# Hybrid decoder block on one core: the order of state output, query rotation and z products, and 64-row matmuls of two group halves taken in turn

## The chip, the cores and the metric

One core of a Trainium2 chip runs the whole program. The metric is the device time of one execution in microseconds; the kernel before was executed three times. Engines are named as in the profile: PE is TensorE (PEld its weight loads), DVE is VectorE, ACT is ScalarE, POOL is GpSimd, SP is SyncE, which here only issues DMA.

## What is computed

One layer over 1024 tokens of width 1024, with two parallel token mixers, in float32:

```
h = rms_norm(x) * (1 + scale) + shift
q | kv(cmp, slc, win) | nsa gates | z_attn | u | z_ssm | merge gates = h @ w_in
A = NSA(rope(q), kv) * silu(z_attn)      # compressed + selected + window attention, 8 heads, 2 KV groups
S = GLU(gelu(S5(u))) * silu(z_ssm)       # 16 SSM groups of 16 channels, 64 complex states each
m = sigmoid(m_a) * (A @ w_proj_attn) + sigmoid(m_s) * (S @ w_proj_ssm)
out = rms_norm(x + gate * (m @ w_out))
```

S5 is a diagonal complex recurrence. The kernel computes it in chunks of 8 tokens: lag kernels (`klag`) give what a token takes from its own chunk, and a scan over 128 chunks gives the state that a chunk starts from. The output y of a group is the state part (real and imaginary) plus the part from within the chunk (a Toeplitz matrix `toep` built from the lags).

## The kernel before, in words

Every engine has its own instruction list, and semaphores tie them together. An engine works its list strictly in order, so the place of a step in the list decides what it can delay. The projections `h @ w_in` are cut into nine weight chunks (U_, ZS_, Q0_, Q1_, KC_, Z0_, KS_, KW_, Z1_, line 56) and eight token tiles of 128 rows. One such unit is 24 matmuls (three products of a high/low split over 8 slices of the width) into one of the banks 4 to 7, and a unit waits until the unit four places before it has been read.

The middle of the program runs in this order on PE: `ZS_`, six tiles of `Q0_`, the lag kernels (lines 1714 to 1724), transposes of the input matrices into `gt` (1726), the last two tiles of `Q0_`, the chunk inputs `bu` (1736), `Q1_`, and then the list `KC_ORDER` (466): units of KC_ and Z0_, mixed with `y` (`lag_outputs`, 1748), its transposes `yt`, key transposes `kc` and the GLU. Fills of banks 0 and 1 are counted: fill n waits (`fill_free`) until the one two places before it has been evicted, which ACT reports on `s_trf`.

In the lag kernels and in y a group pair lies on the partitions: half `gp` = 0 on rows 0 to 63, half 1 on rows 64 to 127. The fp32 matmuls of a fill all use one half, and the profile shows two records for each matmul.

- ACT evicts klag (904), gt, then `b_r` and `b_i` (919 to 926). `b_i` shares its memory with klag, so it waits for the `toep` transfers that SP issues once POOL has added the skip term (`lags`, 716 to 721). Later ACT evicts y to `ytok` (932) and works `KC_READS` (983): values of the KC_ tiles, Gelus of the transposed y, and so on.
- DVE rotates the queries (`rotate_queries`, two heads and half of the tiles a call) for b = 0 and 1 ahead of the state chain (`states`, 1237) and for b = 2 and 3 behind it. `states` is a chain of products of 128x1024 and sixteen scans; with its sixth step lies the low part of the KC_ weights. Its last instruction signals `rot`, on which PE waits for y. `kc_keys` comes behind the last rotation and behind y.
- POOL splits the Z0_ weights (`split_w(5)`, 731) as soon as ACT has their high part.

The attention stage is a written list of steps (`opening_plan`, 135, and `attention_plan`, 149) which every engine works through, each doing its own part of a step. In the opening, `GS` is ACT's sigmoid of the gates, `Z i` the unit i of Z1_ with ACT's silu into `zs`, `KT` key transposes with ACT's and DVE's evictions, `MQ 0` the query transposes of head 0 and ACT's copies into `q1`, `PQ` ACT's scaled copy of a head's queries and POOL's duplicate, `PL` their low part on DVE, `MX` and `MW` the row maxima. `MX` needs `q1` and z unit 1. Per head there are six results (branch br, half cc, r = 2 br + cc). DVE forms each (`ND`); for r of 2 and more POOL adds it into `qa` (783). After every eight of these sums, that is after heads 1, 3 and 5, POOL multiplies a pair of heads with silu(z), 128x1024 (784 to 788). Its queue also holds the low part of the weights of the compressed branch (770).

```
KC_ORDER = [("P", KC_, 0), ("P", KC_, 1), ("y",), ("P", KC_, 2), ("yt", 0), ("yt", 1), ("P", KC_, 3),
...
KC_READS = [step for step in KC_ORDER if step != ("P", KC_, 4)]
KC_READS.insert(KC_READS.index(("kc", 3)) + 1, ("P", KC_, 4))
```

Of the kernel before, what the change touches and what calls it, by code (L numbers as in the profile page):

```python
# [22 lines left out]
P = 128  # L23
SEQ = 1024
D_MODEL = 1024
KT = D_MODEL // P
# [17 lines left out]
CH = 8  # L44
# [90 lines left out]
def opening_plan():  # L135


    def pair(i):
        return [("MX", 0, i), ("MW", 0, i)]
    plan = [("GS",), ("Z", 0, 0, KT), ("KT", 2 * ST - 2), ("KT", 2 * ST - 1), ("PL", 0), ("MQ", 0, 0), ("MQ", 0, 1),  # L140
            ("PQ", 1), ("Z", 1, 0, KT)]
    for i in range(ST):
        plan += pair(i) + [("Z", 2 + i // 2, 4 * (i % 2), 4 * (i % 2) + 4)]
    plan += [("MC", 0, p) for p in range(4)]
    plan += [("Z", 6, 0, KT), ("MM", 0, 0), ("Z", 7, 0, KT), ("MM", 0, 1), ("PL", 1)]
    return plan
# [57 lines left out]
def build(nc, x, c, w_ada, b_ada, norm_gain, w_in, pe_cmp_k, w_cmp_k1, b_cmp_k1, w_cmp_k2,  # L204
# [258 lines left out]
    for n, name in enumerate(FILLS):  # L463
        first.setdefault(name, n)

    KC_ORDER = [("P", KC_, 0), ("P", KC_, 1), ("y",), ("P", KC_, 2), ("yt", 0), ("yt", 1), ("P", KC_, 3),
                ("yt", 2), ("yt", 3), ("P", KC_, 4), ("kc", 0), ("kc", 1), ("glu", 0), ("kc", 2), ("kc", 3),
# [14 lines left out]
    with nc.Block() as block:  # L482
# [114 lines left out]
        def _(pool):  # L597
# [128 lines left out]
            def split_w(w):  # L726

                n = CHUNKS[w][1]
                pool.wait_ge(s_whi, w + 1)
                tt(wlo[w % 2][:, :, 0:n], wraw[:, :, 0:n], f(whi[w % 2][:, :, 0:n]), ALU.subtract).then_inc(s_wlo, 1)  # L730
            split_w(5)
# [19 lines left out]
            for step in [("PQ", 0)] + plan:  # L751
# [20 lines left out]
                elif step[0] == "ND" and step[2] == 3 and step[1] % 6 >= 2:  # L772
# [11 lines left out]
                    if n_sum % 8 == 0 and n_sum < 4 * HEADS:  # L784
                        pool.wait_ge(once("norm"), n_sum)
                        b = n_sum // 8 - 1
                        tt(qa[:, b, :, :], qa[:, b, :, :], zs[:, :, P * b:P * b + P], ALU.mult).then_inc(once("az"), 1)
                        pool.wait_ge(once("az"), b + 1)
# [22 lines left out]
        def _(act):  # L811
# [92 lines left out]
            for q in range(4):  # L904
                gp, th = divmod(q, 2)
                bk = fill(first["klag"] + q)
                a(kl[:, gp, 4 * th:4 * th + 4, :], bk[0:SC, :].rearrange("p (t s) -> p t s", t=4)).then_inc(s_trf, 1)
# [24 lines left out]
            for q in range(4):  # L932
                bk = fill(first["y"] + q)
                if q == 0:
                    act.wait_ge(once("rot"), 1)
                gp, th = divmod(q, 2)
# [199 lines left out]
        def _(dve):  # L1136
# [123 lines left out]
            for b in range(2):  # L1260
                for hf in range(2):
                    rotate_queries(b, slice(4 * hf, 4 * hf + 4))
# [5 lines left out]
            for b in range(2, 4):  # L1268
# [315 lines left out]
        def _(pe):  # L1584
# [129 lines left out]
            for q in range(4):  # L1714
                gp, th = divmod(q, 2)
                n = first["klag"] + q
                fill_free(n)
                s = slice(SS * gp, SS * gp + SS)
                for m in range(4):
                    t = 4 * th + m  # L1720
                    for r in range(2):
                        ins = mm(bank[n % 2][0:SC, P * m:P * m + P], bbar[r][s, t, :],
                                 cp[r][s, t, 0:CH, :].rearrange("p j c -> p (j c)"), r == 0, r == 1)
                ins.then_inc(s_tr, 1)
# [23 lines left out]
            def lag_outputs():  # L1748
# [3 lines left out]
                for q in range(4):  # L1752
                    n = first["y"] + q
                    fill_free(n)
                    gp, th = divmod(q, 2)
                    s = slice(SS * gp, SS * gp + SS)
                    for m in range(4):
                        t = 4 * th + m
                        g = 2 * t + gp
                        o = bank[n % 2][:, P * m:P * m + P]  # L1760
                        for r, st in enumerate((zr, zi)):
                            mm(o, st[s, t, :], cp[r][s, t, 1:9, :].rearrange("p j c -> p (j c)"), r == 0, False)
                        ins = mm(o, ut[:, g, :], toep[:, g, :], False, True)
                    ins.then_inc(s_tr, 1)
# [238 lines left out]
            for step in plan:  # L2003
                if step == ("N", 6 * HEADS - 1):
# [3 lines left out]
                    for n in range(6):  # L2008
                        b, hf = divmod(n, 2)
                        pe.wait_ge(once("az"), b + 1)  # L2010
# [95 lines left out]
```

## Time and profile before

| what | value |
|---|---|
| median of 3 runs | 1028.67 us (1028.46 to 1030.15) |
| the profiled execution | 1029.62 us, its span 1027.7 us |
| PE busy | 943.4 us, 92% of the span |
| DVE, ACT, POOL busy | 529.9, 395.5, 213.3 us |
| mean granted TensorE clock | 0.963 |
| chain that ended last, by engine | PE 74%, DVE 14%, ACT 8%, issue 3% |

The span runs from the first to the last instruction. The chain of the last row follows the program back from its end: at each step to what released the instruction, or to the one before it on its engine. A granted clock of 1.00 is 2.4 GHz, 0.50 is 1.2 GHz. Times in the rows are microseconds from the start of the span.

### The profile page before, as it was taken

Reading aid. Unit: us, or ns where it says so; the run is one execution under the profiler, and the core shown is the slowest. Engines: PE = TensorE matmul, PEld = TensorE weight load, DVE = VectorE, ACT = ScalarE, POOL = GpSimd, SP = SyncE. Lnnn points to the kernel's source line nnn. Section 1 sums busy time; section 2 is a strip of 40 time slices with the busy share of each in tenths; the row PEclk is TensorE's granted clock in tenths of the full one; section 3 lists DMA queues with packets and bytes.
Section 4 is the critical chain, followed back from the end, with each engine's and each line's share of the span. In section 5 each row is a group of like instructions: output and inputs, shape, how many; then the busy total and the mean of one; then the engine's idle time right before and its main releaser. Section 6 shows DMA issues by size and latency. Waiting matters only on the chain.

```text
span 1027.7 us, 14338 instructions
## 1 busy us (share of the span) xinstructions
PE 943.4 (92%) x5581; PEld 770.2 (75%) x5581; DVE 529.9 (52%) x1075; ACT 395.5 (38%) x786; POOL 213.3 (21%) x204
## 2 busy tenths in 40 slices
PE   0799998999998989989989989879999999998996
PEld 0488997879998966666767666568888888886885
DVE  1652198134685466877867868562123122217453
ACT  5542231233114167667666675751111111105121
POOL 6259411012010012122021131135553000000000
PEclk9899997599999999999999999989999999999999
DMA  9916041004110000000000000032332222042322
GB/s 319 327 59 106 7 104 62 1 1 86 41 43 1 1 1 2 1 1 1 2 1 1 1 1 5 27 105 72 96 84 60 57 57 57 1 163 87 119 82 82
DMA packets 53714, 59.66 MB, mean 58 GB/s; under 512 B 10096, under 2 KB 45488, under 8 KB 52608
## 3 DMA queue, kind: packets, MB, share of 16 engines
q1 hardware_dynamic: 51392, 54.13, 17.7%
q0 software_dynamic: 2000, 4.54, 1.6%
q8 instruction: 44, 0.72, 0.3%
q14 instruction: 22, 0.18, 0.1%
q10 hardware_dynamic: 256, 0.09, 0.0%
HBM read 52.92 MB, written 5.24 MB: 57 GB/s over the span
## 4 chain that ended last, share of the span: by engine, by line
PE 74%; DVE 14%; ACT 8%; issue 3%; DMA 1%; POOL 0%; ACTq 0%; DVEq 0%
PE bank L1588 42%; PE slc_max L1588 15%; PE win_max L1588 13%; PE bank L1591 3%; DVE plo L1141 3%; DVE mx L1410 2%; ACT pt L815 1%; DVE mx L1417 1%; ACT phi L815 1%; ACT osb L815 1%; DVE zi L1141 1%; DVE rt L1141 1%; ACT L815 1%; ACT junk L815 1%; DMA prow<-in_lam_im 1%
## 5 line engine op out<-in xcount | busy, mean ns | idle before, releaser
L1141 DVE TENSOR_TENSOR plo<-pt,phi 128x512 fp32r<-128x512 f32 x192 | 117.1, 626 | 40.1 <-ACT phi L815 39.7
L815 ACT ACTIVATE pt<-bank 128x512 f32<-128x512 f32 (+1 forms) x208 | 98.7, 475 | 92.1 <-PE bank L1588 91.0
L1588 PE MATMUL bank<-q,k 128*128 128x512 f32 (+7 forms) x384 | 104.0, 353 | 0.9
L815 ACT ACTIVATE phi<-bank 128x512 fp32r<-128x512 f32 (+1 forms) x208 | 98.4, 473 | 0.0
L601 POOL TENSOR_TENSOR qa<-qa,otmp 128x256 f32<-128x256 f32 x32 | 27.7, 865 | 221.4 <-DVE otmp L1141 221.4
L1588 PEld LDWEIGHTS bank<-q,k 128*128 128x128 f32 (+1 forms) x384 | 64.3, 192 | 12.3 <-ACT phi L815 3.3
L1588 PE MATMUL bank<-phi,vhi 128*65 128x512 f32 x192 | 71.0, 370 | 2.3 <-ACT osb L815 1.9
L1588 PE MATMUL bank<-phi,vlo 128*64 128x512 f32 x192 | 62.9, 328 | 0.0
L1588 PE MATMUL bank<-plo,vhi 128*65 128x512 f32 x192 | 62.9, 328 | 0.0
L1410 DVE TENSOR_REDUCE mx<-slc_max 128x1 f32<-128x128 f32 (+3 forms) x64 | 48.1, 752 | 13.1 <-PE slc_max L1588 13.1
L1588 PE MATMUL bank<-ht_hi,dhi 128*128 128x512 f32 x128 | 51.0, 398 | 2.4 <-DVE at_lo L1141 2.4
L1588 PE MATMUL bank<-ht_hi,dlo 128*128 128x512 f32 x128 | 50.8, 397 | 0.0
L1588 PE MATMUL bank<-ht_lo,dhi 128*128 128x512 f32 x128 | 50.8, 397 | 0.0
L815 ACT ACTIVATE dsig<-bank 128x512 f32<-128x512 f32 x16 | 9.6, 599 | 106.3 <-PE bank L1588 106.3
L1588 PE MATMUL bank<-whi,ht_hi 128*128 128x256 f32 (+1 forms) x160 | 47.9, 299 | 0.0
L1588 PE MATMUL bank<-wlo,ht_hi 128*128 128x256 f32 (+1 forms) x160 | 46.4, 290 | 0.0
L1588 PE MATMUL win_max<-whi,ht_hi 128*128 128x256 f32 (+1 forms) x160 | 46.3, 290 | 0.0
L1588 PE MATMUL bank<-whi,ht_lo 128*128 128x256 f32 (+1 forms) x160 | 46.3, 289 | 0.0
L1588 PE MATMUL win_max<-wlo,ht_hi 128*128 128x256 f32 (+1 forms) x160 | 45.4, 284 | 0.0
L1588 PE MATMUL win_max<-whi,ht_lo 128*128 128x256 f32 (+1 forms) x160 | 45.2, 283 | 0.0
L1417 DVE TENSOR_REDUCE mx<-win_max 128x1 f32<-128x640 f32 (+2 forms) x64 | 41.5, 648 | 0.0
L1141 DVE TENSOR_TENSOR mt<-bank,dsig 128x512 f32<-128x512 f32 x8 | 5.5, 692 | 64.4 <-ACT dsig L815 54.4
(385 smaller groups left out, 2595.8 us busy)
## 6 DMA issues: line engine op xcount, KB each, us to landing
ada<-in_w_ada SPq DMA_DIRECT2D x8, 1024.0 KB, 17.3
draw<-in_w_in SPq DMA_DIRECT2D x16, 512.0 KB, 3.9
wraw<-in_w_in SPq DMA_DIRECT2D x7, 1024.0 KB, 6.0
xs<-in_x SPq DMA_DIRECT2D x8, 512.0 KB, 11.1
gstage<-in_w_ada POOLq DMA_DIRECT2D x16, 256.0 KB, 3.1
oraw<-in_w_out SPq DMA_DIRECT2D x8, 512.0 KB, 6.6
xr<-in_x SPq DMA_DIRECT2D x8, 512.0 KB, 4.3
out<-yr SPq DMA_DIRECT2D x8, 512.0 KB, 2.9
```

Of the source, the lines that this page charges most:

```text
L601: return nc.gpsimd.tensor_tensor(o, a, b, op)
L815: return nc.scalar.activation(o, i, fn, **kw)
L1141: return V.tensor_tensor(o, a, b, op)
L1410: V.tensor_reduce(m[:, i, 1:2], slc_max[:, 0:P * (i + 1)], AX.X, ALU.max).then_inc(once("msr"), 1)
L1417: V.tensor_reduce(m[:, i, 2:3], win_max[:, 0:P * min(i + 1, WIN_TILES + 1)], AX.X, ALU.max)\
L1588: return T.matmul(o, l, r, start=start, stop=stop, **kw)
L1591: return T.transpose(o, i, ident[0:rows, 0:rows])
```

## The change

- `KC_ORDER`: y comes after three KC_ tiles instead of two, and its transposes one tile later too.
- POOL waits for `rot` before it splits the Z0_ weights.
- DVE rotates only b = 0 ahead of the states, and b = 1 to 3 behind them.
- Lag kernels and y: the two halves gp take turns, instruction by instruction, and each half and th has a bank of its own (0 to 3). ACT evicts in the new order. In y the eight 128-row matmuls with `toep` follow the sixteen 64-row ones of their th.
- POOL's z product is done in pieces of 128x256, each right behind a window sum (r of 4 and 5) of heads 0 to 5.
- Opening: z unit 1 comes before the query steps of head 0.

```diff
--- before.py
+++ after.py
@@ -137,8 +137,8 @@
 
     def pair(i):
         return [("MX", 0, i), ("MW", 0, i)]
-    plan = [("GS",), ("Z", 0, 0, KT), ("KT", 2 * ST - 2), ("KT", 2 * ST - 1), ("PL", 0), ("MQ", 0, 0), ("MQ", 0, 1),
-            ("PQ", 1), ("Z", 1, 0, KT)]
+    plan = [("GS",), ("Z", 0, 0, KT), ("KT", 2 * ST - 2), ("KT", 2 * ST - 1), ("PL", 0), ("Z", 1, 0, KT), ("MQ", 0, 0),
+            ("MQ", 0, 1), ("PQ", 1)]
     for i in range(ST):
         plan += pair(i) + [("Z", 2 + i // 2, 4 * (i % 2), 4 * (i % 2) + 4)]
     plan += [("MC", 0, p) for p in range(4)]
@@ -463,8 +463,8 @@
     for n, name in enumerate(FILLS):
         first.setdefault(name, n)
 
-    KC_ORDER = [("P", KC_, 0), ("P", KC_, 1), ("y",), ("P", KC_, 2), ("yt", 0), ("yt", 1), ("P", KC_, 3),
-                ("yt", 2), ("yt", 3), ("P", KC_, 4), ("kc", 0), ("kc", 1), ("glu", 0), ("kc", 2), ("kc", 3),
+    KC_ORDER = [("P", KC_, 0), ("P", KC_, 1), ("P", KC_, 2), ("y",), ("P", KC_, 3), ("yt", 0), ("yt", 1), ("P", KC_, 4),
+                ("yt", 2), ("yt", 3), ("kc", 0), ("kc", 1), ("glu", 0), ("kc", 2), ("kc", 3),
                 ("P", KC_, 5), ("glu", 1), ("P", KC_, 6), ("glu", 2), ("P", KC_, 7), ("glu", 3),
                 ("P", Z0_, 0), ("kc", 4), ("kc", 5), ("P", Z0_, 1), ("kc", 6), ("kc", 7)]
     KC_ORDER += [("P", Z0_, i) for i in range(2, ST)]
@@ -728,6 +728,7 @@
                 n = CHUNKS[w][1]
                 pool.wait_ge(s_whi, w + 1)
                 tt(wlo[w % 2][:, :, 0:n], wraw[:, :, 0:n], f(whi[w % 2][:, :, 0:n]), ALU.subtract).then_inc(s_wlo, 1)
+            pool.wait_ge(once("rot"), 1)
             split_w(5)
 
             for n in range(4):
@@ -781,11 +782,10 @@
                     n_sum += 1
                     dst = qa[:, h // 2, 4 * cc:4 * cc + 4, HD * (h % 2):HD * (h % 2) + HD]
                     tt(dst, dst, otmp[:, :, :], ALU.add).then_inc(once("norm"), 1)
-                    if n_sum % 8 == 0 and n_sum < 4 * HEADS:
+                    if r >= 4 and h < HEADS - 2:
                         pool.wait_ge(once("norm"), n_sum)
-                        b = n_sum // 8 - 1
-                        tt(qa[:, b, :, :], qa[:, b, :, :], zs[:, :, P * b:P * b + P], ALU.mult).then_inc(once("az"), 1)
-                        pool.wait_ge(once("az"), b + 1)
+                        tt(dst, dst, zs[:, 4 * cc:4 * cc + 4, HD * h:HD * h + HD], ALU.mult).then_inc(once("az"), 1)
+                        pool.wait_ge(once("az"), 2 * h + cc + 1)
 
             pool.wait_ge(once("norm"), 4 * HEADS)
             for n in range(2 * KT):
@@ -902,9 +902,9 @@
                 query_tile(Q0_, i)
             kl = klag[:, :, :].rearrange("p (t g) s -> p g t s", g=2)
             for q in range(4):
-                gp, th = divmod(q, 2)
-                bk = fill(first["klag"] + q)
-                a(kl[:, gp, 4 * th:4 * th + 4, :], bk[0:SC, :].rearrange("p (t s) -> p t s", t=4)).then_inc(s_trf, 1)
+                th, gp = divmod(q, 2)
+                fill(first["klag"] + q)
+                a(kl[:, gp, 4 * th:4 * th + 4, :], bank[q][0:SC, :].rearrange("p (t s) -> p t s", t=4)).then_inc(s_trf, 1)
             for q in range(4):
                 r, th = divmod(q, 2)
                 bk = fill(first["gt"] + q)
@@ -930,10 +930,11 @@
                 query_tile(Q1_, i)
             split_w(Z0_)
             for q in range(4):
-                bk = fill(first["y"] + q)
+                fill(first["y"] + q)
+                bk = bank[q]
                 if q == 0:
                     act.wait_ge(once("rot"), 1)
-                gp, th = divmod(q, 2)
+                th, gp = divmod(q, 2)
                 yv = ytok[:, :, :].rearrange("p j (t g c) -> p g t j c", g=2, c=SC)
                 a(yv[:, gp, 4 * th:4 * th + 4, :, :], bk.rearrange("p (t j c) -> p t j c", t=4, c=SC)).then_inc(s_trf, 1)
 
@@ -1257,15 +1258,14 @@
                 yield ch.link(tt(zI, zI, eC, ALU.mult))
                 yield tt(zI, zI, bI, ALU.add).then_inc(once("rot"), 1)
 
-            for b in range(2):
-                for hf in range(2):
-                    rotate_queries(b, slice(4 * hf, 4 * hf + 4))
+            for hf in range(2):
+                rotate_queries(0, slice(4 * hf, 4 * hf + 4))
             dve.wait_ge(s_trf, first["bu"] + 4)
             dve.wait_ge(once("ecos"), 1)
             for n, _ in enumerate(states()):
                 if n == 6:
                     split_w(KC_)
-            for b in range(2, 4):
+            for b in range(1, 4):
                 for hf in range(2):
                     rotate_queries(b, slice(4 * hf, 4 * hf + 4))
 
@@ -1711,17 +1711,15 @@
             project(Q0_, range(6))
             pe.wait_ge(once("cp"), 1)
             pe.wait_ge(s_eva, UU)
-            for q in range(4):
-                gp, th = divmod(q, 2)
-                n = first["klag"] + q
-                fill_free(n)
-                s = slice(SS * gp, SS * gp + SS)
+            for th in range(2):
                 for m in range(4):
                     t = 4 * th + m
                     for r in range(2):
-                        ins = mm(bank[n % 2][0:SC, P * m:P * m + P], bbar[r][s, t, :],
-                                 cp[r][s, t, 0:CH, :].rearrange("p j c -> p (j c)"), r == 0, r == 1)
-                ins.then_inc(s_tr, 1)
+                        for gp in range(2):
+                            s = slice(SS * gp, SS * gp + SS)
+                            ins = mm(bank[2 * th + gp][0:SC, P * m:P * m + P], bbar[r][s, t, :],
+                                     cp[r][s, t, 0:CH, :].rearrange("p j c -> p (j c)"), r == 0, r == 1)
+                ins.then_inc(s_tr, 2)
             pe.wait_ge(once("gs"), 2)
             for q in range(4):
                 r, th = divmod(q, 2)
@@ -1749,19 +1747,20 @@
 
                 pe.wait_ge(once("rot"), 1)
                 pe.wait_ge(once("toep"), 16 * CH)
-                for q in range(4):
-                    n = first["y"] + q
-                    fill_free(n)
-                    gp, th = divmod(q, 2)
-                    s = slice(SS * gp, SS * gp + SS)
+                pe.wait_ge(s_trf, first["y"])
+                for th in range(2):
                     for m in range(4):
                         t = 4 * th + m
-                        g = 2 * t + gp
-                        o = bank[n % 2][:, P * m:P * m + P]
                         for r, st in enumerate((zr, zi)):
-                            mm(o, st[s, t, :], cp[r][s, t, 1:9, :].rearrange("p j c -> p (j c)"), r == 0, False)
-                        ins = mm(o, ut[:, g, :], toep[:, g, :], False, True)
-                    ins.then_inc(s_tr, 1)
+                            for gp in range(2):
+                                s = slice(SS * gp, SS * gp + SS)
+                                mm(bank[2 * th + gp][:, P * m:P * m + P], st[s, t, :],
+                                   cp[r][s, t, 1:9, :].rearrange("p j c -> p (j c)"), m == 0 and r == 0, False)
+                    for gp in range(2):
+                        for m in range(4):
+                            g = 2 * (4 * th + m) + gp
+                            ins = mm(bank[2 * th + gp][:, P * m:P * m + P], ut[:, g, :], toep[:, g, :], False, m == 3)
+                        ins.then_inc(s_tr, 1)
 
             def lag_transposes(q):
 
@@ -2007,7 +2006,7 @@
                     pe.wait_ge(once("exp"), 2 * HEADS * NU)
                     for n in range(6):
                         b, hf = divmod(n, 2)
-                        pe.wait_ge(once("az"), b + 1)
+                        pe.wait_ge(once("az"), 4 * (b + 1))
                         for q in range(4):
                             ins = tr(bank[n][:, P * q:P * q + P], qa[:, b, 4 * hf + q, :])
                         ins.then_inc(once("att"), 1)
```

## Rows read from the trace of the kernel before

**Rows 1.** PE in order of time, the state outputs y (start, us, engine, line, operation).

```profile
166.13 0.48 PE L1588 MATMUL bank<-cp,zr 64*128 64x128 f32 x2 [4.29 <-DVE zi L1141]
...
171.36 0.79 PE L1588 MATMUL bank<-cp,zr 64*128 64x128 f32 x2
...
173.23 0.79 PE L1588 MATMUL bank<-cp,zr 64*128 64x128 f32 x2
```

**Rows 2.** DVE in order of time, state chain, rotations, first two KC_ tiles.

```profile
138.95 1.23 DVE L1141 TENSOR_TENSOR zr<-b_r,ecos 128x1024 f32<-128x1024 f32 x1
...
158.94 5.87 DVE L1141 TENSOR_TENSOR zi<-zi,ecos 128x1024 f32<-128x1024 f32 x1
...
165.99 0.75 DVE L1141 TENSOR_TENSOR rt<-qa,rope 128x256 f32<-128x256 f32 x2
...
195.88 0.49 DVE L1141 TENSOR_TENSOR rt<-win_max,rope 128x128 f32<-128x128 f32 x2 [19.68 <-PE bank L1588]
...
196.93 0.49 DVE L1141 TENSOR_TENSOR rt<-win_max,rope 128x128 f32<-128x128 f32 x2
```

**Rows 3.** Windows: stretch, length, busy us of PE PEld DVE ACT POOL, PEclk, DMA.

```profile
194.00:196.00 2.00, 2.00 (x8) 1.78 (x9) 0.12 (x1) 0.18 (x1) 0.00 (x0) 0.50 0.00 0
457.00:458.00 1.00, 1.00 (x4) 0.66 (x2) 0.96 (x3) 0.00 (x0) 0.00 (x0) 0.50 0.00 0
```

**Rows 4.** The chain that ended last, in order of time (start, us, what).

```profile
122.75 5.70 PE bank L1588 x48
...
209.71 3.44 PE slc_max L1588 x8
```

**Rows 5.** PE in order of time, the opening of the attention stage.

```profile
331.02 1.94 PE L1591 MATMUL bank<-ident,qc 128*128 128x128 f32 x8 [2.96 <-DVE k L1471]
...
336.90 0.30 PE L1588 MATMUL slc_max<-k,q 128*128 128x128 f32 x1 [0.63 <-issue]
```

**Rows 6.** POOL in order of time, heads 1 to 3.

```profile
410.92 0.73 POOL L601 TENSOR_TENSOR qa<-qa,otmp 128x256 f32<-128x256 f32 x1 [4.97 <-DVE otmp L1141]
...
441.43 1.29 POOL L601 TENSOR_TENSOR phi<-pt,phi 64x512 fp32r<-64x512 f32 x1 [1.37 <-ACT phi L815]
...
449.33 0.73 POOL L601 TENSOR_TENSOR qa<-qa,otmp 128x256 f32<-128x256 f32 x1 [4.96 <-DVE otmp L1141]
450.14 2.38 POOL L601 TENSOR_TENSOR qa<-qa,zs 128x1024 f32<-128x1024 f32 x1
...
491.19 0.73 POOL L601 TENSOR_TENSOR qa<-qa,otmp 128x256 f32<-128x256 f32 x1 [4.98 <-DVE otmp L1141]
```

**Rows 7.** DVE in order of time, the subtraction behind the second window sum.

```profile
412.07 0.69 DVE L1141 TENSOR_TENSOR plo<-pt,phi 128x512 fp32r<-128x512 f32 x1
...
450.48 2.59 DVE L1141 TENSOR_TENSOR plo<-pt,phi 128x512 fp32r<-128x512 f32 x1
```

**Rows 8.** PE in order of time, lag kernels, gt, bu.

```profile
113.33 6.74 PE L1588 MATMUL bank<-cp,bbar 64*16 64x128 f32 x64
120.00 2.75 PE L1591 MATMUL bank<-ident,gs 128*128 128x128 f32 x16
...
128.36 1.97 PE L1588 MATMUL bank<-ut,gt 128*64 128x128 f32 x32
```

**Rows 9.** ACT in order of time, state inputs, y, Gelus.

```profile
135.50 1.08 ACT L815 ACTIVATE b_i<-bank 128x508 f32<-128x508 f32 x2 [3.79 <-DMA toep<-klag]
...
195.82 0.60 ACT L815 ACTIVATE ytok<-bank 128x512 f32<-128x512 f32 x1 [6.90 <-PE bank L1588]
...
201.84 1.28 ACT L815 ACT_TABLE_LOAD   x1
203.13 2.15 ACT L815 ACTIVATE yt<-bank 128x512 f32<-128x512 f32 x2
```

**Rows 10.** POOL in order of time, the split of the Z0_ weights.

```profile
158.64 5.09 POOL L601 TENSOR_TENSOR wlo<-wraw,whi 128x2240 fp32r<-128x2240 f32 x1 [24.67 <-ACT whi L815]
```

**Rows 11.** PE in order of time, head 1, transposes of a result.

```profile
414.50 0.43 PE L1591 MATMUL bank<-ident,osb 65*128 65x65 f32 x4 [0.58 <-DVE qa L1141]
```

## The prediction, made before the change was built

> **What bounds the kernel now.** I read the chain that ended last, then the waits of each engine, then the timelines of the stretches the diff touches. TensorE carries three quarters of the chain, so what counts is where it idles or runs at half clock. Three places show both.
>
> First, the state stage. TensorE waits 4.29 us for VectorE's last state product, starts the outputs y at 166.13 [rows 1], and the last of y lets VectorE go on at 195.88 [rows 2]: 29.7 us. The granted clock there is 0.50, the 1.2 GHz level [rows 3]; the six instructions of one group come every 1.87 us, while the first two, right behind the wait, took 0.33 [rows 1]. Work behind y reaches the first GLU matmuls at 209.71 [rows 4].
>
> Second, the opening of the attention stage: TensorE waits 2.96 us for VectorE's key copy, then does eight query transposes in 1.94 us, and the first maxima start at 336.90 [rows 5].
>
> Third, the heads. POOL's second window sum of a head comes at 410.92, 449.33 and 491.19: 38.41 us apart, but 41.86 where a 128x1024 z product follows the sum [rows 6]. That product holds VectorE's subtraction for 2.59 us instead of 0.69 [rows 7], and later the clock is at 0.50 [rows 3]. The whole excess of 3.45 us reaches the next head, three times in the kernel.
>
> **Part 1, lag kernels (klag).** 64 instruction records of 64 rows took 6.74 us, 0.105 each [rows 8]. The new order alternates the two 64-row halves in separate banks. No row shows row halves side by side; the nearest is bu, which alternates the two column halves: 32 records in 1.97 us, 0.062 each [rows 8]. The bounds are 0.062 (3.9 us) and 0.105 (6.7 us); I take 3.9, as only bu has TensorE switch halves between neighbours. It ends at 117.3 instead of 120.1. But both banks of a pair are now handed over at once, and the gt transposes wait for the third eviction (0.60 like any 512-column one [rows 9]); TensorE waits 0.65 us, and gt alternates with evictions, ending near 120.6 instead of 122.75: 2.1 us gained. With no overlap the same wait loses 0.65. SP's toep transfers, queued behind these lags, move with it, and with them ScalarE's b_i copy, which waits for them [rows 9].
> The Trainium skill (TensorEngine Tiling (Array Packing), Key Properties and Gotcha 1) says that different tiles of the array work in parallel and that two row tiles may not use one PSUM bank at once. By it klag would take half, 3.4 us; no row here shows it for row tiles.
>
> **Part 2, states earlier and undisturbed.** Today the state chain starts at 138.95 [rows 2], behind four head rotations of tile pair b=1. These cost 10.21 us for eight (165.99 to 195.88 less the 19.68 idle [rows 2]), 1.28 each, 5.1 together; without them VectorE is free at 133.8. The b_i copies now start at 135.50 and take 1.08 [rows 9]; 2.1 earlier they end at 134.5. So the states start 4.2 us earlier. In the chain one product took 5.87 instead of 1.23 us [rows 2], while POOL split the z weights for 5.09 us [rows 10]. POOL will wait for the states, so 4.6 goes. States end near 166.1 - 4.2 - 4.6 = 157.3. What is late next: the split now falls on the rotations, which grow from 8 to 12 (15.3 us) plus 5.0 of blocking, ending at 177.6. Behind POOL's new wait stands, on its own queue, only the GLU gating, whose input comes after the GLU matmuls; SP's next weight load waits for the split, which ends near 162.4, 1.3 us sooner.
>
> **Part 3, y one tile later.** TensorE reaches y now at 161.8 and waits; then it comes 2.1 earlier plus one projection tile (2.85, half of [rows 4]): 162.6, five us after the states. No wait, so no fall of the clock from that cause. At full clock a y record costs 0.156 (half of 1.87/6; the first pair gives 0.165): 96 make 15.0; with the 64 of 64 rows cheaper in the ratio 0.062 to 0.105 of part 1, 10.9. Bounds: 10.9 and 29.7. I take 10.9, so y ends at 173.5. Then the queue is no longer TensorE's: the first KC tile can be rotated at 177.6, each tile costs 1.05 (195.88 to 196.93 [rows 2]), so the fourth is read at 181.3 and copied by ScalarE at 181.7. Only then, since four tiles now stand ahead of the Gelu, come the table load of 1.28 and four Gelus at 2.15 a pair [rows 9]: 187.3. With the last transposes the GLU matmuls start at 187.8 instead of 209.71: 21.9 gained. On the way TensorE idles twice: the next tile and two transposes end at 177.4, but the bank of the tile after comes free at 178.5; that tile ends at 181.4, and the next transposes wait for the first Gelu, done at 184.1 (2.7 us, as long as the 2.96 before which the opening lost its clock [rows 5]). So I expect half clock into the first GLU block: 3.44 us [rows 4] would at worst double; I charge half, 1.7. Gain: 20.2. The faster y itself is mostly hidden behind VectorE and ScalarE.
>
> **Part 4, opening.** The 24 matmuls of z tile 1 (2.85) fill the 2.96 wait, so the transposes stay at 331.0 but run at full clock, 1.0 instead of 1.94. ScalarE's silu for that tile goes ahead of the query copies and fits before them. Two copies of about 0.55 follow the transposes; the maxima start near 332.85 instead of 336.90: 4.0 gained. If the clock fell all the same, 3.1.
>
> **Part 5, z product in pieces.** Three big products go: 3 x 3.45 = 10.35. Twelve pieces come, two per head in six heads. The piece behind the second sum: a free 128x256 sum took 0.73 [rows 6], so it runs 411.73 to 412.46 and meets the subtraction that starts at 412.07 [rows 7]. Under the big product the subtraction ended 0.55 behind POOL; so it ends at 413.01 instead of 412.76, 0.25 late. TensorE already waits 0.58 us on that VectorE chain [rows 11], so this passes through: 6 x 0.25 = 1.5. Bounds: a piece of 0.60 (a quarter of 2.38) gives 0.12, one of 0.98 gives 0.5: 0.7 to 3.0. The piece behind the first sum lies in POOL's 1.37 us idle ahead of the next subtraction [rows 6]; cost nothing, or 0.7 a head if the phi values came sooner. Net 8.9.
> The Trainium skill (SBUF — State Buffer, the reading of the port diagram) says the pair shared by VectorE and GpSimd is locked for a whole instruction. That speaks against this part, as six more heads collide; by it a piece costs its remaining time, and the trace agrees with 2.59 us.
>
> **Sum.** 20.2 + 4.0 + 8.9 = 33.1 us. The profiled execution took 1029.62 (span 1027.7, the rest around it), the median is 1028.67, 0.95 less. 1028.67 - 33.1 = 995.5.
>
> **Rivals.**
> A: row halves do not overlap, clock kept. For it: no row shows overlap. TensorE reaches y at 165.3, y ends at 180.3, the tile, copy, table and Gelus then give GLU at 190.3; no idle, so no clock loss. Gain 19.4 + 12.9 = 32.3: 996.4. It differs in y's rows more than in the time.
> B: the clock falls in y although nothing was waited for, as it did not recover there in 29 us of busy TensorE [rows 3]. Against: it stayed full through klag and bu. Overlapped, y takes 21.8 and ends at 184.4, the next two tiles 5.7 each, the Gelus follow, and GLU starts at 199.5: gain 10.2 + 12.9 = 23.1, 1005.6. Not overlapped, y takes 7.9 more: 1013.5.
> C, the slower one: each change of row half empties the array. It decides from 32.3 / 128 = 0.25 us per change in klag and y. A y pair record lasts 0.79 us from start to end [rows 1]; if each record took that at half clock (0.40 in klag), klag grows by 18.6, y to 60.6, GLU starts near 252: 1058. Against: bu changes column halves at 0.062.
> D: the instructions take no advantage and the waits reappear (states bound by the toep transfers, say). Then only parts 4 and 5 remain: 1015.8.
>
> **Chances.** Mine 0.62, A 0.13, B 0.15, C 0.04, D 0.05, nothing changed 0.01. A measurement can tell some 0.2% (2 us) from no change. The range: best case, no clock loss (1.7) and pieces at their cheapest (0.8), some margin for klag: 990.5; worst, B overlapped: 1005.5. B serial, C, D lie outside. Faster 0.94, same 0.02, slower 0.04.
>
> **What would show it.** klag in 3.9 us or 6.7; states' end near 157 with no 5.87 product; the 5 us block among the rotations; y starting with no wait at full clock; GLU at 188; maxima near 332.9 of old time; heads all 38.66 apart. Wrong if the clock is 0.50 in y, if ScalarE's Gelus come later than VectorE's rotations explain, or if each head shows a TensorE wait far over 0.8 us and half clock behind it.

## The result and the profile after

The changed kernel takes 991.16 us, median of four runs (990.72 to 992.08), against 1029.41 (1028.46 to 1030.52) for the kernel before: ratio 0.9629, 95% interval 0.9613 to 0.9646. The profiled execution took 991.09 us, its span 989.3, against 1029.62 and 1027.7.

The page of the changed kernel (busy time of TensorE; its clock in 40 slices; the chain that ended last):

```profile
PE 910.2 (92%) x5573; PEld 745.6 (75%) x5581; DVE 528.5 (53%) x1075; ACT 394.5 (40%) x786; POOL 215.7 (22%) x213
PEclk9999999899999999999999999989999999999998
PE 71%; DVE 14%; ACT 6%; SPq 3%; issue 3%; DMA 2%; POOL 0%; DVEq 0%; ACTq 0%; POOLq 0%
```

TensorE lost 33 us of busy time, though it does the same matmuls: its mean granted clock rose from 0.963 to 0.987, and the 64-row records overlap, which shortens the lags from 6.74 to 3.66 us and y, at full clock, from 16.7 (only_order, below) to 7.8. To see where, I measure every stage from the first lag record, since the part ahead of it, which the change doesn't touch, ended at 113.33 us before and 111.92 after (111.1 to 113.2 in the other runs below). GLU's first record stands at 209.55 in the timeline before (the chain's row in [rows 4] begins at 209.71).

| stage, us | before | after | gain | predicted |
|---|---|---|---|---|
| first lag record to GLU's first | 96.2 | 73.4 | 22.8 | 21.9 |
| GLU to the first maxima | 127.35 | 123.46 | 3.9 | 4.0 less 1.7 |
| first maxima to the last window sum | 340.61 | 331.61 | 9.0 | 8.9 |
| ahead of the lags, and behind the last sum | | | 2.7 | 0 |

The gains are 38.4 us, the difference of the spans. The 1.7 is what the prediction charged for a GLU at half clock. Of the last row 1.4 is the start and 1.3 lies behind the last sum, in code that is the same. By the mean granted clock of the 12 us there (from 678 before, from 641 after), TensorE was at half clock for 10.2 us before and for 6.8 after. The other runs go with it: those with 6.8 take 349.0 to 349.7 us from the last sum to the end, those with 10.2 take 350.1 to 350.6.

**Lags and states.** PE, ACT, DVE and POOL of the changed kernel in order of time (start, duration, engine, line, operation, count, idle time before and its releaser):

```profile
111.92 1.92 PE L1588 MATMUL bank<-cp,bbar 64*16 64x128 f32 x32
113.67 1.91 PE L1588 MATMUL slc_max<-cp,bbar 64*16 64x128 f32 x32
116.36 1.06 PE L1591 MATMUL bank<-ident,gs 128*128 128x128 f32 x8 [0.78 <-ACT klag L815]
131.51 1.08 ACT L815 ACTIVATE b_i<-bank 128x508 f32<-128x508 f32 x2 [3.73 <-DMA toep<-klag]
132.66 0.07 DVE L1241 MEMSET b_r<- 128x8 f32 x1 [3.54 <-ACT b_i L815]
154.03 1.22 DVE L1142 TENSOR_TENSOR zi<-zi,b_i 128x1024 f32<-128x1024 f32 x1
155.18 5.58 DVE L1142 TENSOR_TENSOR rt<-qa,rope 128x256 f32<-128x256 f32 x2
155.34 5.13 POOL L601 TENSOR_TENSOR wlo<-wraw,whi 128x2240 fp32r<-128x2240 f32 x1 [25.31 <-DVE zi L1142]
```

The 64 lag records take 3.66 us, 0.057 each, instead of 6.74 [rows 8]. The 5.87 us product of [rows 2] is gone from the states, and the 5 us block has moved behind them. New is VectorE's wait of 3.54 us for b_i: the time that the moved rotations used to fill.

**y and what follows.** PE, then DVE and ACT, in order of time:

```profile
160.66 0.49 PE L1588 MATMUL bank<-cp,zr 64*128 64x128 f32 x4
168.43 0.36 PE L1588 MATMUL bank<-whi,ht_hi 128*128 128x256 f32 x1
176.55 0.55 PE L1588 MATMUL win_max<-whi,ht_hi 128*128 128x256 f32 x1 [4.16 <-ACT catc L815]
182.06 0.66 PE L1591 MATMUL bank<-ident,ytok 128*128 128x128 f32 x4
185.36 1.02 PE L1588 MATMUL slc_max<-yt,wglu 128*128 128x512 f32 x2
175.50 0.49 DVE L1142 TENSOR_TENSOR rt<-win_max,rope 128x128 f32<-128x128 f32 x2
179.19 0.38 ACT L815 ACTIVATE catc<-bank 128x256 f32<-128x256 f32 x1 [0.67 <-DVE rt L1142]
179.59 1.28 ACT L815 ACT_TABLE_LOAD   x1
180.88 3.93 ACT L815 ACTIVATE yt<-bank 128x512 f32<-128x512 f32 x4
```

And the windows behind y (stretch, length, busy us of PE PEld DVE ACT POOL, PEclk, DMA share, GB/s):

```profile
176.00:178.00 2.00, 1.45 (x7) 1.48 (x8) 1.73 (x6) 0.77 (x2) 0.00 (x0) 0.50 0.00 0
180.00:182.00 2.00, 1.99 (x10) 1.71 (x9) 0.00 (x0) 1.99 (x3) 0.00 (x0) 0.54 0.00 0
182.00:184.00 2.00, 1.32 (x8) 0.85 (x9) 0.00 (x0) 2.00 (x4) 0.00 (x0) 1.00 0.00 0
```

y starts without a wait and takes 7.8 us (160.66 to 168.43) instead of 29.7. But TensorE then idles 4.16 us for a bank that VectorE's rotations hold back, falls to half clock, and is back at full clock before GLU.

**Opening and heads.** PE, POOL and DVE in order of time, head 0 and the sum of head 1:

```profile
306.81 1.07 PE L1591 MATMUL bank<-ident,qc 128*128 128x128 f32 x8
308.82 0.33 PE L1588 MATMUL slc_max<-k,q 128*128 128x128 f32 x1 [0.94 <-ACT q L815]
382.81 0.73 POOL L601 TENSOR_TENSOR qa<-qa,otmp 128x256 f32<-128x256 f32 x1 [4.96 <-DVE otmp L1142]
383.62 0.73 POOL L601 TENSOR_TENSOR qa<-qa,zs 128x256 f32<-128x256 f32 x1
383.96 0.94 DVE L1142 TENSOR_TENSOR plo<-pt,phi 128x512 fp32r<-128x512 f32 x1
386.64 0.44 PE L1591 MATMUL bank<-ident,osb 65*128 65x65 f32 x4 [0.83 <-DVE qa L1142]
421.45 0.73 POOL L601 TENSOR_TENSOR qa<-qa,otmp 128x256 f32<-128x256 f32 x1 [4.95 <-DVE otmp L1142]
```

The transposes run at full clock without a wait (1.07 us for eight, 1.94 in [rows 5]). The second window sums of heads 0 to 5 are now 38.63 to 38.67 us apart; the subtraction takes 0.94 instead of 0.69, and TensorE waits 0.83 instead of the 0.58 of [rows 11].

### The profile page after: what moved, and what is told of

The parts are those of the page before. It is cut to its first block, busy times and chain, and to the rows that moved or that the text cites. A ratio compares the mean times of both kernels' runs of the same rounds, so it can differ in the third digit from the quotient of the medians.

```text
span 989.3 us, 14340 instructions
## 1 busy us (share of the span) xinstructions
PE 910.2 (92%) x5573; PEld 745.6 (75%) x5581; DVE 528.5 (53%) x1075; ACT 394.5 (40%) x786; POOL 215.7 (22%) x213
## 4 chain that ended last, share of the span: by engine, by line
PE 71%; DVE 14%; ACT 6%; SPq 3%; issue 3%; DMA 2%; POOL 0%; DVEq 0%; ACTq 0%; POOLq 0%
PE bank L1588 39%; PE slc_max L1588 15%; PE win_max L1588 13%; PE bank L1591 3%; DVE plo L1142 3%; SPq L488 2%; DVE rt L1142 2%; DVE mx L1410 2%; DMA ada<-in_w_ada 2%; ACT pt L815 1%; DVE mx L1417 1%; ACT phi L815 1%; ACT osb L815 1%; DVE qa L1142 1%; SPq L527 1%
## 6 DMA issues: line engine op xcount, KB each, us to landing
xs<-in_x SPq DMA_DIRECT2D x8, 512.0 KB, 10.9
```

## The experiments

"GLU" is from the first lag record to GLU's first, in the one profiled execution of each kernel. The times are medians of 4 to 6 runs; each group was timed with the kernel before on the same chip, whose median was 1027.7 to 1029.1.

| run | time, us | GLU |
|---|---|---|
| before | 1029.41 | 96.2 |
| the full change | 991.16 (990.72 to 992.08) | 73.4 |
| only_zpieces | 1018.00 (1017.22 to 1021.61) | 96.1 |
| only_opening | 1022.33 (1020.29 to 1024.59) | 96.2 |
| only_turns | 1006.33 (1005.14 to 1008.09) | 71.2 |
| only_order | 1009.14 (1005.88 to 1011.76) | 78.2 |
| no_order | 990.67 (990.02 to 991.93) | 71.2 |
| undo_poolwait | 992.01 (990.97 to 992.85) | 73.6 |
| y_serial | 996.91 (993.71 to 999.06) | 74.0 |
| klag_serial | 995.15 (993.87 to 996.50) | 75.7 |
| split_later | 988.20 (987.61 to 988.77) | 69.4 |
| later_no_order | 984.70 (984.00 to 985.87) | 66.5 |
| z_later | 990.75 (989.88 to 992.10) | 73.4 |
| combination | 983.01 (982.60 to 987.19) | 66.5 |

### One part of the change at a time, on the kernel before

Only the z product in pieces:

```diff
-                    if n_sum % 8 == 0 and n_sum < 4 * HEADS:
+                    if r >= 4 and h < HEADS - 2:
...
+                        tt(dst, dst, zs[:, 4 * cc:4 * cc + 4, HD * h:HD * h + HD], ALU.mult).then_inc(once("az"), 1)
```

> The kernel before with the z product in pieces alone. Theory (a piece holds the shared port for its rest, 0.25 us a head): every head 38.64 to 38.66 us, the three long heads gone, 9.0 us faster. Rival (something else in the change shortens the heads too, e.g. the clock): clearly less than 9 here.

Ratio 0.9907 (0.9880 to 0.9934), 11 us for the 9.0 expected. Heads 0 to 5 are 38.62 to 38.65 us apart, as expected, but the gain is not all theirs. From the first maxima to the last sum the profile gains 6.5 us and not 9.0, as the clock was down in the last heads, where it was not in the full change (a window, columns as above). It gains 1.3 us in the opening, where the wait of 2.96 us left the clock at 1.00 this time, and 1.9 ahead of the lags:

```profile
633.00:642.00 9.00, 8.15 (x32) 5.97 (x33) 4.21 (x13) 4.61 (x12) 1.15 (x2) 0.62 0.01 2
```

Only the opening:

```diff
-    plan = [("GS",), ("Z", 0, 0, KT), ("KT", 2 * ST - 2), ("KT", 2 * ST - 1), ("PL", 0), ("MQ", 0, 0), ("MQ", 0, 1),
-            ("PQ", 1), ("Z", 1, 0, KT)]
+    plan = [("GS",), ("Z", 0, 0, KT), ("KT", 2 * ST - 2), ("KT", 2 * ST - 1), ("PL", 0), ("Z", 1, 0, KT), ("MQ", 0, 0),
+            ("MQ", 0, 1), ("PQ", 1)]
```

> The kernel before with z unit 1 ahead of the query steps alone. Theory (the unit fills the wait for VectorE's key copy and holds the clock): 3.9 us faster, query transposes at full clock. Rival (only the clock is gained, the unit just moves): about 1 us.

Ratio 0.9947 (0.9929 to 0.9965). The maxima come 3.9 us earlier, as in the full change. The rest was not expected: two of the three long heads are 40.3 us long and not 41.9. TensorE waits behind the big product as before (its row in order of time), but keeps its clock (the window behind it); behind the third big product, after a wait of 2.50 us, it fell again.

```profile
450.78 0.43 PE L1591 MATMUL bank<-ident,osb 65*128 65x65 f32 x4 [2.48 <-DVE qa L1141]
```

```profile
452.00:458.00 6.00, 6.00 (x42) 4.17 (x42) 5.77 (x16) 3.48 (x8) 0.00 (x0) 1.00 0.00 0
```

In the kernel before, a wait of the same length (2.47) was followed by 0.50 [rows 3]. No edit touches the code of these heads, so this part of the gain came with the clock and is not the work of the edit; a wait alone does not tell whether it falls.

Only the turns of the row halves, in their own banks, with the 128-row matmuls of y behind the 64-row ones:

```diff
+                        for gp in range(2):
+                            s = slice(SS * gp, SS * gp + SS)
+                            ins = mm(bank[2 * th + gp][0:SC, P * m:P * m + P], bbar[r][s, t, :],
...
-                        ins = mm(o, ut[:, g, :], toep[:, g, :], False, True)
+                    for gp in range(2):
+                        for m in range(4):
+                            g = 2 * (4 * th + m) + gp
```

> The kernel before with the two row halves taking turns in klag and y alone, y still behind two tiles and behind the wait. Theory 1 (row halves in separate banks overlap at either clock, and here nothing hides y, since VectorE idles 19.7 us behind it): klag 3.6 us and what follows 2.5 earlier, y at half clock 16 us instead of 29.7, in all 14 to 17 us faster. Theory 2 (the turns bring nothing, y was short in the changed kernel by its clock alone): within 1 us of the kernel before.

Ratio 0.9792 (0.9769 to 0.9816), some 23 us, far more than expected. PE in order of time, first record of each half of y, and the windows of the first six us:

```profile
163.41 0.80 PE L1589 MATMUL bank<-cp,zr 64*128 64x128 f32 x4 [4.29 <-DVE zi L1142]
168.78 0.49 PE L1589 MATMUL slc_max<-cp,zr 64*128 64x128 f32 x4
```

```profile
163.00:166.00 3.00, 2.59 (x24) 2.59 (x26) 2.79 (x8) 0.00 (x0) 0.00 (x0) 0.50 0.38 114
166.00:169.00 3.00, 3.00 (x31) 2.76 (x31) 2.79 (x8) 0.71 (x2) 0.00 (x0) 0.94 1.08 380
```

TensorE still waits 4.29 us and still falls to 0.50, but is back at full clock after 3 us, where it stayed at 0.50 through the whole y before. y takes 9.2 us (163.41 to 172.57). Of the 25.0 us gained at GLU 2.5 are lost in the heads: two of the long ones take 43.1 and 43.3 us instead of 41.9, as the clock stayed at 0.50 for 6.8 us in them and not for 3.4 (by the mean granted clock behind the wait). The run changes three things at once, the turns, the banks and the place of the 128-row matmuls; no run shows which of them brings the clock back.

Only the order (rotations of b = 1 behind the states, y one tile later, POOL's wait):

```diff
-    KC_ORDER = [("P", KC_, 0), ("P", KC_, 1), ("y",), ("P", KC_, 2), ("yt", 0), ("yt", 1), ("P", KC_, 3),
+    KC_ORDER = [("P", KC_, 0), ("P", KC_, 1), ("P", KC_, 2), ("y",), ("P", KC_, 3), ("yt", 0), ("yt", 1), ("P", KC_, 4),
...
+            pool.wait_ge(once("rot"), 1)
...
-            for b in range(2, 4):
+            for b in range(1, 4):
```

> The kernel before with the order alone: y behind three tiles, one tile pair rotated ahead of the states, POOL's split behind them; klag and y one half after the other as before. Theory (y's clock comes from the missing wait, and VectorE and ScalarE set when the GLU starts): states done near 159.4, y at full clock in about 15 us, GLU near 190 of 209.7, 19 to 20 us faster. Rival (the faster y is what counts): under 12 us faster.

Ratio 0.9817 (0.9779 to 0.9855). With no wait in front of it, the old y keeps full clock to its end (PE in order of time):

```profile
162.55 0.48 PE L1588 MATMUL bank<-cp,zr 64*128 64x128 f32 x2
163.19 0.49 PE L1588 MATMUL bank<-toep,ut 128*128 128x128 f32 x2
163.61 0.48 PE L1588 MATMUL bank<-cp,zr 64*128 64x128 f32 x2
```

Six records come every 1.06 us and the 96 take 16.7: it was the clock that made y 29.7 us long. Either part alone ends the long stretch at half clock in y, which is why their gains at GLU (25.0 and 18.0 us) don't add: together they give 22.8, less than the turns alone.

### One part left out or altered, on the full change

Without the order part:

```diff
-    KC_ORDER = [("P", KC_, 0), ("P", KC_, 1), ("P", KC_, 2), ("y",), ("P", KC_, 3), ("yt", 0), ("yt", 1), ("P", KC_, 4),
+    KC_ORDER = [("P", KC_, 0), ("P", KC_, 1), ("y",), ("P", KC_, 2), ("yt", 0), ("yt", 1), ("P", KC_, 3),
...
-            pool.wait_ge(once("rot"), 1)
...
-            for b in range(1, 4):
+            for b in range(2, 4):
```

> The full change without its reordering part (query rotations, KC order and POOL's wait as before); alternating row halves, opening and z pieces stay. Theory (with the row halves alternating, the reordering brings nothing, since VectorE's rotations behind the states are then the chain): GLU starts 71 to 72 us after the first lag record, as in the run with the alternation alone (71.2), against 73.4 in the full change, so 1 to 2.5 us faster than the full change: 988.5 to 990. Rival 1 (the reordering still pays, as it keeps the clock and frees the states of the z split): GLU starts later than 73.4, 992 to 996. Rival 2: the fall of the clock in y comes back through the earlier start after a VectorE wait and stays, 1000 or more.

990.67 against 991.16: GLU comes 2.2 us sooner, as expected, but the time is above the 988.5 to 990 expected, and the two medians can't be told apart. Its profile starts the lags 0.9 us later and gives 1.4 us back behind the last window sum, where the code is the same and TensorE was at half clock for 10.2 us instead of 6.8. So the order part brings nothing once the halves take turns; in the stage that it touches it costs 2.2 us. The reason stands in two rows of DVE:

```profile
135.42 0.42 DVE L1141 TENSOR_TENSOR qa<-rt,rt 128x256 f32<-128x256 f32 x1
135.92 1.23 DVE L1141 TENSOR_TENSOR zr<-b_r,ecos 128x1024 f32<-128x1024 f32 x1
```

Here VectorE has no gap ahead of the states; they start 23.1 us after the first lag record. In the full change they start at 20.9, 2.2 sooner, but 5.1 us of rotations then stand behind them, on the chain to the KC_ tiles.

Without POOL's wait:

```diff
-            pool.wait_ge(once("rot"), 1)
             split_w(5)
```

> The full change without POOL's wait for the states. Theory (the 5 us block moves from the rotations back into the states: same VectorE chain, same sum): the states end some 4.5 us later (one product of about 5.9), the rotations end where they did; y starts near 165 and takes 8 us, to about 173, still ahead of the tile that is rotated at 175.4; the time stays within 1 us of 991.2, and TensorE's idle time moves from behind y to in front of it. Rival 1: the wait is worth its 4.6 us: 995.8. Rival 2: the idle time in front of y costs the clock in y: 993 to 996.

No difference, and not by the way I gave. DVE and POOL:

```profile
153.18 1.23 DVE L1141 TENSOR_TENSOR zi<-zi,b_i 128x1024 f32<-128x1024 f32 x1
154.32 5.24 DVE L1141 TENSOR_TENSOR rt<-qa,rope 128x256 f32<-128x256 f32 x1
153.91 5.37 POOL L601 TENSOR_TENSOR wlo<-wraw,whi 128x2240 fp32r<-128x2240 f32 x1 [24.66 <-ACT whi L814]
```

ScalarE delivers the weights at 153.9, when the last product of the states is already running, and that product takes its 1.23 us. The block falls on the rotations as it does with the wait. The wait guards the states against a collision that their earlier start had already ended.

y and the lags one half after the other, in the same banks:

```diff
-                    for m in range(4):
-                        t = 4 * th + m
-                        for r, st in enumerate((zr, zi)):
-                            for gp in range(2):
+                    for gp in range(2):
+                        for m in range(4):
+                            t = 4 * th + m
+                            for r, st in enumerate((zr, zi)):
```

(and the same for the lags, in klag_serial).

> The full change, but the 64-row records of y run one half after the other in each pair of banks (klag still alternates). Theory (y's speed is hidden behind VectorE's rotations and the 4.16 us for which TensorE idles behind it): y grows by about 2.7 us, from 8.0 to about 10.7, the idle time shrinks by as much, GLU starts as before (73.4 after klag's first record) and the time stays within 0.5 us: 991. Rival: y's length passes through, or the idle time that is left decides over the clock: plus 2.5 to 3, 994, or, with less idle and no fall of the clock, minus 1 to 2.

> The full change, but the 64 lag records run one half after the other, in the same four banks. Theory (the lags stand on the chain through the toep transfers to the states): klag takes about 6.7 us instead of 3.66, everything behind it moves by 3.0: 994.2. Rival (separate banks are the gain and not the alternation): klag stays at 3.7 and the time at 991.2. Rival 2 (the states have slack): klag 6.7, time within 1 us of 991.2.

PE in order of time, the two waits behind y in y_serial, then the lags in klag_serial:

```profile
176.74 0.35 PE L1588 MATMUL win_max<-whi,ht_hi 128*128 128x256 f32 x1 [1.28 <-ACT catc L815]
182.21 2.05 PE L1591 MATMUL bank<-ident,ytok 128*128 128x128 f32 x8 [2.39 <-ACT yt L815]
```

```profile
111.53 2.92 PE L1588 MATMUL bank<-cp,bbar 64*16 64x128 f32 x29
114.29 0.27 PE L1588 MATMUL bank<-cp,bbar 64*16 64x128 f32 x1
114.30 0.27 PE L1588 MATMUL slc_max<-cp,bbar 64*16 64x128 f32 x1
114.52 2.91 PE L1588 MATMUL slc_max<-cp,bbar 64*16 64x128 f32 x29
```

Separate banks alone give little: the lags take 5.9 us (6.74 before, 3.66 with turns), and what they save lies at the changes of half, where records of both halves run side by side (114.29 and 114.30); y takes 10.6. In y_serial TensorE idles twice (1.28 and 2.39) instead of once (4.16), and GLU comes only 0.6 us later, near what the theory said. Yet its median is 5.7 us higher. The profiled execution was its fastest (993.71), 2.6 above that of the full change: 0.6 at GLU, and 1.7 behind the last sum, where TensorE was at half clock for 10.2 us and not 6.8. The others took 995.06 to 999.06, at a mean granted clock of 0.986 to 0.979 instead of 0.988, so they spent more time at half clock. Where, and whether the slower y is the reason, no profile shows. That stays open. In klag_serial the gt transposes and GLU come 2.2 and 2.3 us later, so the lags stand on the chain; its profiled execution took 993.87, 2.8 more than that of the full change, and its median is 4.0 higher.

### Towards a faster kernel

POOL's split behind the fourth rotated KC_ tile, on the full change and on no_order:

```diff
-            pool.wait_ge(once("rot"), 1)
+            pool.wait_ge(once("kcat"), 4)
             split_w(5)
```

> The full change, with POOL's split of the z weights put off until four KC tiles are rotated (kcat 4) instead of until the states are ready. Theory (VectorE's chain from the states to the fourth KC tile sets the start of GLU, and the 5 us block is part of it): the rotations end near 170.4 instead of 175.4, the fourth tile is copied near 174.2, TensorE's idle of 4.16 us behind y shrinks below 1, the clock stays full, and GLU starts near 180, 68 to 69 us after klag's first record instead of 73.4: 986 to 987. Rival 1 (behind the states another limit is close, ScalarE's Gelus or the blocked KC tiles): GLU 1 to 2 us earlier only, 989 to 990. Rival 2 (the split, now late, holds the later KC tiles or the weight load queued behind it): no gain or a loss, 991 to 995.

> The same delay of POOL's split, but on the kernel without the reordering part (rotations and KC order as before). Theory (the reordering is worth nothing by itself; what counts is that the split is off VectorE's chain): states end about 4.6 us earlier than there, y starts near 158.5 with little wait, GLU starts 66.5 to 68.5 after klag's first record (71.2 with the split in the states): 985.5 to 987. Rival (once the split is gone, the order decides, since TensorE waits in front of y here and loses its clock): 989 to 991, clearly behind the run with both.

ACT's table load and PE's wait in order of time, with the window behind it, of split_later, then the same rows of later_no_order:

```profile
175.83 1.28 ACT L815 ACT_TABLE_LOAD   x1
178.28 0.66 PE L1591 MATMUL bank<-ident,ytok 128*128 128x128 f32 x4 [2.26 <-ACT yt L815]
```

```profile
180.00:182.00 2.00, 1.73 (x8) 1.53 (x9) 0.00 (x0) 1.73 (x3) 0.89 (x1) 0.50 0.01 1
```

```profile
171.95 1.28 ACT L815 ACT_TABLE_LOAD   x1
174.39 0.66 PE L1592 MATMUL bank<-ident,ytok 128*128 128x128 f32 x4 [0.85 <-ACT yt L815]
```

With the block gone, the order part costs 3.5 us: 988.20 with it, 984.70 without. In split_later all four KC_ tiles stand ahead of the table load and the Gelus, TensorE has nothing left in its list to do before the next transposes, idles 2.26 us and loses its clock. In later_no_order the fourth tile comes between the transposes, the table is loaded behind the third tile, and the clock stays at 1.00. Splitting later is worth 3.0 us on the full change and 6.0 without the order.

The second z piece of each head behind the next head's first sum:

```diff
-                    if r >= 4 and h < HEADS - 2:
+                    due = [(h, 0)] if r == 4 and h < HEADS - 2 else []
+                    if r == 2 and h >= 1 and h - 1 < HEADS - 2:
+                        due = [(h - 1, 1)]
```

> The full change, but the second z piece of each head no longer follows its own window sum: it follows the next head's first sum, so that it no longer meets VectorE's subtraction. Theory (the collision costs 0.25 us in each of six heads, as the heads are 38.65 apart instead of 38.41): heads 38.41 apart and the time 1.5 us lower, 989.7. Rival (the piece that is moved now sits in front of another POOL step of the chain, two pieces behind one sum): heads stay at 38.65 or grow, 991 to 993.

DVE and PE in order of time, behind the second sum of head 0:

```profile
384.11 0.69 DVE L1146 TENSOR_TENSOR plo<-pt,phi 128x512 fp32r<-128x512 f32 x1
386.54 0.43 PE L1595 MATMUL bank<-ident,osb 65*128 65x65 f32 x4 [0.60 <-DVE qa L1146]
```

The subtraction is back at 0.69, the wait at 0.60, the heads 38.4 apart: the last sum comes 1.5 us sooner from the opening on. The median falls by 0.4 only, and the two ranges overlap; the profile loses 0.8 us of it again behind the last sum and 0.2 ahead of the lags.

Both together, without the order part:

> The kernel without the reordering part, with POOL's split behind the fourth KC tile, and with the second z piece of each head behind the next head's first sum. Theory (the two fixes are in different stages and add): GLU 66.5 us after klag's first record, heads 38.4 apart, 984.7 - 1.5 = 983.2. Rival (what is saved in the heads is lost behind them, where the profile of the moved piece alone lost 0.6 us again): 984.1 to 984.7.

983.01, as the sum said: 0.9583 (0.9558 to 0.9608) of the kernel before, and 8 us below the changed kernel.

## Why the prediction was right, and where it was not

Predicted were 995.5 (990.5 to 1005.5), measured 991.16; of 38.3 us gained, 33.1 were foreseen.

**Part 1** held: 3.66 us for 3.9. The Trainium skill (TensorEngine Tiling (Array Packing), Key Properties) has different tiles working in parallel; the rows agree, 0.057 against 0.105 us a record, and klag_serial shows that the turns do it.

**Part 2** had the numbers right and the reading wrong. The states ended at 155.25, which is 156.7 in the times of the kernel before, whose lags start 1.4 later, for 157.3, and the block appeared among the rotations. But I booked 4.6 us for POOL's wait where undo_poolwait shows none: I counted the collision at its old place without asking whether the earlier states still meet the split. That the sum held there is luck: the block left the states because they run earlier, with or without the wait. I also had VectorE free at 133.8, 0.7 ahead of b_i. It was free 3.54 ahead of it, mostly since the rotations that stay came 2.5 us sooner behind the shorter lags. So I didn't set the 5.1 us of moved rotations against the idle time that they leave.

**Part 3** failed in two terms. The 1.7 us for a half-clock GLU was not paid: the clock fell behind y, and was back by 182. The chain itself was about 1 shorter (73.4 for 74.5). The idle time I gave as two waits of 1.1 and 2.7 us; it came as one of 4.16, since y took 7.8 and not 10.9; the tile behind it, at half clock, took 5.4 us and filled the second. In y the 128-row records, grouped behind the 64-row turns, come at 0.125 each, where I had scaled the mixed rate of 0.156.

**The parts were not priced apart.** The prediction let the order carry the gain and called the faster y mostly hidden. Within the full change y_serial bears that out at GLU (0.6 us for a y 2.9 us longer). But the turns alone bring 25.0 us there, and with them in, the order costs 2.2. That the change as a whole came out near the sum doesn't show that the order earned it.

**The step behind rival B was false.** It took the 29 us at 0.50 [rows 3] as a sign that the clock doesn't hold or recover in y. only_order shows that the old y holds full clock when nothing was waited for, and only_turns that the new y is back at it after 3 us. The rival took a chance of 0.15 and the whole upper end of the range. Rivals A (no overlap) and C (a cost for each change of half) are excluded by the lag records, D by the 22.8 us at GLU. For A the prediction said that no row shows row halves side by side. The trace of the kernel before does show it, once: at the one change of half in its lags eight records start within 0.35 us (116.39 to 116.74), where elsewhere they are 0.11 apart.

**Parts 4 and 5** held to 0.1 us each, and the price of 0.25 per piece was exact: it went when the piece was moved. By the Trainium skill (SBUF — State Buffer, the reading of the port diagram) the pair is locked for a whole instruction; the row of 0.94 for 0.69, and its end in z_later, agree.

The 2.7 us outside the touched stages were not foreseen and are not the work of the edits: the start wanders by 2 us from run to run, and the half clock behind the last sum lasts 6.8 or 10.2 us.

## What to carry to other kernels

Two parts that both end the same stall must be priced together: alone they were worth 25.0 and 18.0 us at GLU; with the order in, the turns added 4.8, and with the turns in, the order took 2.2 away. Before an instruction is moved out of the way of a late one, look at what its engine does in the gap that is left; and after a stage has moved, ask again whether each guard around it still guards anything. Leave TensorE one independent tile between two steps that wait on other engines.

## What was not expected of the hardware

- The clock's fall does not follow from the length of a wait alone: 2.47 us before one head led to 0.50, 2.48 us before the same head in only_opening left it at 1.00. The 2.96 us before the opening led to 0.50 in the kernel before, only_turns and only_order, and not in only_zpieces. A single wait of 0.85 us left it at 1.00, those of 2.26, 4.16 and 4.29 us did not; but in only_zpieces it fell at 634.9 behind waits of only 0.74 and 0.37 us in head 6, which left it at 1.00 in the full change.
- How long it stays down depends on what TensorE then does. At half clock, y with one half after the other and 128-row records between them stayed at 0.50 for 29 us; the same matmuls, halves in turns and 128-row records apart, were back at 1.00 after 3 us. At full clock the old y kept 1.00 to its end. The 29 us appear in all three runs with the old y behind the wait (before, only_opening, only_zpieces), the 3 us in both with the new y behind it (only_turns, no_order). But the stay also differs where the code is the same: before the same head, behind waits of 2.47 and 2.48 us, it lasted 3.4 us in the kernel before and 6.8 in only_turns.
- Two 64-row halves in separate banks: 0.057 us a record in the lags and 0.062 in y, against 0.092 (klag_serial) and 0.107 (y_serial, 32 records from 160.85 to 164.28) one half after the other in these four banks, and 0.105 before.
